# Hybrid DeltaNet/S5 decoder step: a new PSUM allotment, later norm sums and a finer state chain in the mixer of layer 0

## The reference

```python
proj = (h @ w_in).astype(f32)                       # q, k, v, z, b, a
qkv_c, conv_new = short_conv(qkv, conv0, conv_w)    # 4 taps, then silu
q = l2norm(q); k = l2norm(k)
lmat = jnp.where(strict, einsum(kb, kc) * decay, 0.0)
sol = triangular_solve(eye + lmat, rhs)             # w and u of each chunk
qk = einsum(qc, kc) * decay
def step(S, xs):                                    # over the chunks, in order
    v_new = u_i - w_i @ S
    o = (q_i * exp(g_i)) @ S + qk_i @ v_new
    S = S * exp(g_last) + k_dec.T @ v_new
o = rmsnorm(o, norm_g) * silu(z)
out = o @ w_out                                     # then x = x + out
```

## Time and profile before

| | us |
|---|---|
| median of three runs | 4183.62 (4179.11 to 4185.27) |
| profiled execution, its own time | 4190.18 |
| its span | 4188.5 |
| PE busy over the span | 3619.4 (86%) |
| DVE busy | 2147.4 (51%) |
| ACT busy | 849.4 (20%) |
| mixer of layer 0, from 90 to 2110: PE busy | 1708.4 of 2020 |
| the same stretch: DVE busy | 1160.5 |
| the same stretch: mean granted clock of PE | 0.95 |

### The profile page before, as it was taken

The page is one execution under the profiler, slowest core; times in us unless marked ns, Lnnn a source line. Parts: engine busy times, 40 slices in busy tenths (PEclk is TensorE's granted clock), DMA queues, the critical chain, the costliest instruction groups (busy, mean ns, idle before and its releaser), DMA issues.

```text
span 4188.5 us, 56507 instructions
## 1 busy us (share of the span) xinstructions
PE 3619.4 (86%) x23849; PEld 3490.9 (83%) x23849; DVE 2147.4 (51%) x4331; ACT 849.4 (20%) x1691; POOL 846.0 (20%) x773
## 2 busy tenths in 40 slices
PE   4888888888888888878878999999668979999998
PEld 3878878878788888878868999999648969999997
DVE  2564655656556464655646665755561232333334
ACT  2323222232323223222220101011121020000001
POOL 1201011020101101011012332233232313333331
PEclk8989999999999999999988999999868989999998
DMA  2100000010000001000001122222471101111111
GB/s 73 32 21 28 16 32 32 21 33 16 32 27 28 26 26 33 16 32 32 16 27 37 63 74 79 72 81 63 138 216 53 46 26 46 46 46 49 47 46 56
DMA packets 91964, 197.28 MB, mean 47 GB/s; under 512 B 23232, under 2 KB 51008, under 8 KB 90560
## 3 DMA queue, kind: packets, MB, share of 16 engines
q1 hardware_dynamic: 65344, 152.42, 11.4%
q10 hardware_dynamic: 26368, 41.25, 3.0%
HBM read 152.69 MB, written 40.94 MB: 46 GB/s over the span
## 4 chain that ended last, share of the span: by engine, by line
PE 75%; DVE 18%; ACT 2%; issue 2%; DMA 1%; SPq 0%; POOL 0%; DVEq 0%; ACTq 0%; POOLq 0%
PE ps L210 22%; PE ps L467 12%; PE ps L1133 10%; PE ps L546 5%; PE ps L633 4%; PE ps L619 4%; PE ps L629 4%; PE ps L240 2%; PE ps L491 1%; PE ps L485 1%; DVE dwork L1069 1%; PE ps L595 1%; DVE S L1024 1%; PE ps L479 1%; DVE n_r L1342 1%
## 5 line engine op out<-in xcount | busy, mean ns | idle before, releaser
L210 PE MATMUL ps<-hhi,whi 128*128 128x344 f32 x2520 | 811.5, 322 | 86.5 <-DVE hlo L269 71.8
L210 PE MATMUL ps<-hhi,wlo 128*128 128x344 f32 x2520 | 808.8, 321 | 0.0
L210 PE MATMUL ps<-hlo,whi 128*128 128x344 f32 x2520 | 808.1, 321 | 0.0
L1814 POOL TENSOR_TENSOR wtick<-wtick 128x1 f32<-128x1 f32 x213 | 44.0, 206 | 3136.9 <-PE ps L210 977.1
L210 PEld LDWEIGHTS ps<-hhi,whi 128*128 128x128 f32 x2520 | 477.5, 189 | 90.0 <-issue 65.6
L1817 POOL TENSOR_TENSOR wlo<-wraw,whi 128x1024 fp32r<-128x1024 f32 x213 | 534.0, 2507 | 17.1
L210 PEld LDWEIGHTS ps<-hhi,wlo 128*128 128x128 f32 x2520 | 477.0, 189 | 0.0
L210 PEld LDWEIGHTS ps<-hlo,whi 128*128 128x128 f32 x2520 | 476.5, 189 | 0.0
L1186 DVE TENSOR_TENSOR ab<-ps,sg 128x344 f32<-128x344 f32 x132 | 68.2, 517 | 639.2 <-PE ps L210 627.9
L467 PE MATMUL ps<-hhi,whi 128*128 128x344 f32 x1152 | 386.5, 335 | 7.4 <-DVE olo L889 4.6
L467 PE MATMUL ps<-hlo,whi 128*128 128x344 f32 x1152 | 372.2, 323 | 0.0
(11 more groups left out here) (330 smaller groups left out, 6261.7 us busy)
## 6 DMA issues: line engine op xcount, KB each, us to landing
wraw<-in_w SPq DMA_DIRECT2D x213, 512.0 KB, 3.7
tab<-keep_tab SPq DMA_DIRECT2D x8, 1088.0 KB, 6.8
S<-in_sin ACTq DMA_DIRECT2D x16, 512.0 KB, 3.7
out_sout<-S ACTq DMA_DIRECT2D x16, 512.0 KB, 2.6
keep_u<-hs SPq DMA_DIRECT2D x8, 580.0 KB, 3.2
uu<-keep_u SPq DMA_DIRECT2D x8, 580.0 KB, 8.0
keep_tab<-cp ACTq DMA_DIRECT2D x8, 576.0 KB, 6.3
keep_y<-yg SPq DMA_DIRECT2D x64, 68.5 KB, 2.5
```

Of the source, the lines that this page charges most:

```text
L210: ins = nc.tensor.matmul(out, w, r[:, kt, blk(n)], start=k == 0, stop=k == 3 * KT - 1)
```

## The change

- **Banks.** The whole chain has bank 3, with kS and o in columns 0 to 255 and vn and S in columns 256 to 511. Banks 4, 5, 6 and 7 are one pool: each filler states until which slot it will hold its bank, and `aside` takes the bank that is free first by that estimate. In the dense stage `take` goes round seven banks.
- **Chain.** It has eight steps in place of six: o and S are steps of their own. In a quad they stand in slots 0, 1, 2, 3 and 5, 6, 7, 8. In the dense stage steps 0 to 5 lie in the first projection as before, and 6 and 7 in the second; the last gate sum moves from its second half step to its fifth.
- **Norm sums.** `norm(i, 0)` comes after projection 2 instead of 1, `norm(i, 1)` after 3 instead of 2. On DVE the squares of k come before the convolution of q. ACT evacuates projection 2 before the second silu, and makes each root on its own (`root`).
- **DVE's order in a quad.** The level mask of the next quad (`NM` 1) comes before the last add to Y, and the first half of the sample's state update (`sample_add`, k = 0) before `triangle` in slot 9.
- The end of the mixer is written anew for eight chain steps.

```diff
-        DENSE = (0, 1, 2, 5, 6, 7)
-        CHAIN_SLOT = {0: 0, 2: 1, 4: 2, 5: 3, 7: 4, 8: 5}
+        DENSE = (0, 1, 2, 4, 5, 6, 7)
+        CHAIN_SLOT = {0: 0, 1: 1, 2: 2, 3: 3, 5: 4, 6: 5, 7: 6, 8: 7}
...
-            def aside(who, name):
-                nonlocal side
-                side += 1
-                return use(5 + (side - 1) % 2, who, name)
+            def aside(who, name, free_at):
+                b = min(free, key=lambda k: (free[k], k))
+                free[b] = free_at
+                return use(b, who, name)
...
-                    b = use(4, "DVE", g + f"S{c}")
+                else:
+                    p.after("DVE", g + "kd")
+                    b = use(3, "DVE", g + f"S{c}")
...
-                norm(i, 0)
                 for _ in dense_steps(i, 2):
                     pass
-                norm(i, 1)
+                norm(i, 0)
                 p.after("DVE", f"{i}.tab")
                 p.go(rows(i, 0, take, "DVE", f"{i}.0.diff"), f"{i}.0.row")
                 for _ in dense_steps(i, 3):
                     pass
+                norm(i, 1)
...
-                if s == 9 and q + 1 < NQ:
-                    triangle(i, q + 1)
+                if s == 9:
+                    sample_add(i, q, 0)
+                    if q + 1 < NQ:
+                        triangle(i, q + 1)
...
+                        elif q + 1 < NQ:
+                            level_mask(i, q + 1, 1)
```

More of the change, by code:

```diff
@@ L474, in dense_steps, with gate @@
                     yield
-            def gate(g, w, bank):
+            def gate(g, w, bank=take):
                 p.after("DVE", g + "osq")
@@ L554, in slot, with until @@
                 h = SAMPLE_QUAD.get(q)
+                now = (i * NQ + q) * SLOTS + s
+                def until(d):
+                    return lambda who, name: aside(who, name, now + d)
                 if q and s in CHAIN_SLOT:
@@ L557, in slot @@
                 if s == 1:
-                    b = fixed("DVE", g + "ATT")
+                    b = aside("DVE", g + "ATT", now + 1)
                     for c in range(QCH):
@@ L562, in slot @@
                 if s == 2 and q >= 2:
-                    gate(f"{i}.{q - 2}.", QCH * CH, aside)
+                    gate(f"{i}.{q - 2}.", QCH * CH, until(1))
                 if s == 3 and q + 1 < NQ:
-                    p.go(rows(i, q + 1, fixed, "DVE", f"{i}.{q + 1}.diff"), f"{i}.{q + 1}.row")
+                    p.go(rows(i, q + 1, until(1), "DVE", f"{i}.{q + 1}.diff"), f"{i}.{q + 1}.row")
                 if s == 5 and q == NQ - 1:
-                    gate(f"{i}.{NQ}.", B, aside)
+                    gate(f"{i}.{NQ}.", B, until(2))
                 if s == 5 and h is not None:
@@ L584, in slot @@
                         p.after("ACT", f"{i}.silu3")
[L585 removed]
+                    b = aside("ACT", g + "vb", now)
                     for j in range(4):
@@ L597, in slot @@
                 if s == 11:
-                    b = aside("DVE", g + "kd")
+                    b = aside("DVE", g + "kd", now)
                     for c in range(QCH):
@@ L662, in mix_pe @@
             e = HQK - 1
-            gate(f"{e}.{NQ - 2}.", QCH * CH, aside)
-            for k in range(6):
+            gate(f"{e}.{NQ - 2}.", QCH * CH)
+            for k in range(8):
                 chain(e, NQ - 1, k)
                 out_piece(e, k, 0, take)
-            out_piece(e, 6, 0, take)
-            out_piece(e, 7, 0, take)
-            gate(f"{e}.{NQ - 1}.", QCH * CH, take)
+            gate(f"{e}.{NQ - 1}.", QCH * CH)
             for n in (1, 2):
@@ L692, in silu, with root @@
                 a.go(A.activation(qkv[:, t, :], qkv[:, t, :], AF.Silu), f"{i}.silu{t}")
+            def root(i, j):
+                g = f"{i}."
+                for n in range(NC3):
+                    a.after("PE", g + f"nk{j}.{n}")
+                    a.go(A.activation(sqr[j][:, blk(n)], ps[:, a.bank(g + f"ln{j}.{n}"), 0:NB], AF.Ln, bias=eps_t[:, 0:1]), g + f"ln{j}.{n}")
+                a.after("ACT", g + f"ln{j}.{NC3 - 1}")
+                a.go(A.activation(sqr[j], sqr[j], AF.Exp, scale=-0.5), g + f"nr{j}")
             def gate_r(g, w):
@@ L951, in add_x, with sample_add @@
                 v.go(V.tensor_tensor(x[:, m, blk(n)], ps[:, v.bank(f"{e}.x{m}.{n}"), 0:NB], x[:, m, blk(n)], ALU.add), f"{e}.x{m}.{n}")
+            def sample_add(i, q, k):
+                h = SAMPLE_QUAD.get(q)
+                if h is None:
+                    return
+                v.after("PE", f"{i}.drow{h}.{k}")
+                b = v.bank(f"{i}.snew{h}.{k}")
+                for n in range(4):
+                    c = T + 4 * k + n
+                    v.go(V.scalar_tensor_tensor(S0[:, 4 * k + n], ps[:, b, n * P:(n + 1) * P], qkv[:, 0, c:c + 1], S0[:, 4 * k + n], ALU.mult, ALU.add), f"{i}.snew{h}.{k}")
             def slot(i, q, s):
@@ L1041, in mix_dve @@
                     gate_lo(e, NQ - 1)
+                squares(i, 0)
                 conv(i, 1)
-                for j in range(2):
-                    squares(i, j)
+                squares(i, 1)
                 conv(i, 2)
-                for j in range(2):
-                    v.after("ACT", g + f"nr{j}")
-                    v.go(V.scalar_tensor_tensor(qkv[:, j, :], qkv[:, j, :], 1.0 if j == 0 else float(P) ** -0.5, sqr[j], ALU.mult, ALU.mult), g + f"qn{j}")
-                    if j == 0:
-                        decay(i, 0)
+                unit_norm(i, 0)
+                decay(i, 0)
                 conv(i, 3)
+                unit_norm(i, 1)
                 triangle(i, 0)
```

116 lines of the change are left out of this document (57 added, 59 removed).

## The result

| | before | after |
|---|---|---|
| median of 4 runs, us | 4184.44 (4179.11 to 4185.99) | 3982.14 (3981.48 to 3986.41) |
| profiled execution, us | 4190.18 | 3982.19, span 3980.4 |
| ratio, 95% interval | 1 | 0.9521 (0.9504 to 0.9537) |

The kernel became 4.8% faster; the forecast was 3990 us.

A forecast was written before the change was run, and what follows sets the result against it. PE's own work plus its waits for DVE were taken to bound the kernel. Gains 100.2 + 24.5 + 55 + 16 - 2 = 193.7 us; 4190.2 - 193.7 - 6.6 = 3990 us, 4.6% faster, range 3930 to 4060.

The forecast's parts named there:

- Part 1, norm sums: Head of each pair: waits before the norm sums go, 100.2 us, with no new wait at the Gram product.
- the clock term: Norm sums: without waits their products run at full clock, gain 24.5 us, bounds 0 and 24.5.
- Part 2, waits in the quads: Quads: 177.9 us of waits go, 123 us of new ones come, gain 55 us.
- vn of the first chunk (slot 1) needs X, one slot after kS: Quads: new waits of 1.6 us after quads 0 and 2, 0.5 after quad 1; 3.7 a pair.
- the quads' term: Clock in the quads: half of the 33 us lost in slow stretches comes back, 16 us; bounds 0 and 33.
- Part 3, S in o's bank: Chain: S must wait for ACT's copy of o, 0.38 us, but mask products lie between; cost zero.
- the rival with one bank: Chain: S waits for o's copy in full at all 64 products, 24.6 us more, 4015 us; chance 0.07.
- Part 4, end of the mixer: Once, at the mixer's end: second chunk's kS and last gate sum lose cover, some 1 us each, loss 2 us.
- The 6.6 us by which it was moved down: Whole kernel: the profiled execution before lay 6.6 us above the median, so the forecast was lowered by that.
- DVE in the banks' place in full: Quads: gain neither wait nor clock, bank waits only move to vn or a mask; 4061 us, chance 0.16.
- The slower case: Quads: tight chain, each of 48 vn finds a further 4.4 us DVE queue, 211 us, 4201 us; chance 0.03.
- The rival of 3912 us: Quads: new waits are half of those forecast and the clock stays up; chance 0.17.

The follow-up runs named there:

- e1: Kernel before with only the new order of norm sums, squares, roots and multiplications; banks, chain and masks as before: 4053.41 us, ratio 0.9672.
- e3: Kernel after with ACT issuing the sample state's store behind its copy of the next quad's first transpose, not ahead: 3936.45 us, ratio 0.94.
- e2: Kernel after with the norm part undone; one chain bank, pool of four and new mask order stay: 4114.78 us, ratio 0.9827.
- e5: Kernel after with the edits of both e3 and e4: 3915.91 us, ratio 0.9353.
- e4: Kernel after with vn one slot later in both chunks and the steps behind it moved along: 3964.91 us, ratio 0.9467.
- e10: e9 with the second sample update and its store moved into the next quad, the following load also later: 3881.35 us, ratio 0.9272.
- e9: e5 with PE's first transpose of the next quad moved from slot 11 to slot 0, behind kS: 3886.26 us, ratio 0.9283.

## Why the prediction was right, step by step

**Part 1, norm sums: right, the clock term too small.** The waits went in full (100.2 us), and no new one came before the Gram product. The clock term was 24.5 us, and 56.2 - 30.5 = 25.7 came in the sums themselves; another 16 came around them, see the paragraph on the clock. The upper bound was the one to take: with no gap ahead of them, the six products took 1.90 us where they took 3.81. The first sum of the third pair in the kernel after:

```profile
562.95 1.90 PE L481 MATMUL ps<-dwork,ones 128*128 128x344 f32 x6
```

e1 alone gave 133 us where the two terms of the forecast gave 124.7.

**Part 2, waits in the quads: the sum nearly right, one term wrong.** The new waits were put at 123 us. The list has 43.9 + 37.8 + 20.4 + 19.3 + 7.3 + 4.8 and some 7 us of small ones, 141 (the gate sum's 7.4 us are left out, as nearly all of them lie outside the quads, and so is the single wait of 3.8 us, which is the sixteenth case of the first line: it has the same length and place, in the first pair, and is gone in e3). The terms by themselves, third pair:

| step | predicted | measured |
|---|---|---|
| second sample product | 1.3 | 1.38 |
| first transpose, end of quads 0, 1, 2 | 0.8, 1.7, 0.8 | 0.51, 1.72, 0.22 |
| vn slot 6, quads 1, 2, 3 | 2.2, 1.3, 1.3 | 1.61, 1.30, 1.30 |
| vn slot 1 after quad 1 | 0.5 | 0.44 |
| first sample products | 1.0 | 0.90 |
| vn slot 1 after quads 0 and 2 | 1.6 each | none; instead mask products 2.86 each |

Each of these stands on a line like the following, of the kernel after:

```profile
633.44 1.16 PE L598 MATMUL ps<-ident,sdel 128*128 128x128 f32 x8 [1.38 <-DVE S L972]
...
659.76 0.71 PE L520 MATMUL ps<-dwork 128*128 128x128 f32 x4 [1.61 <-DVE dwork L953]
...
694.74 0.71 PE L520 MATMUL ps<-dwork 128*128 128x128 f32 x4 [1.30 <-DVE dwork L953]
```

The step that failed is "vn of the first chunk (slot 1) needs X, one slot after kS". It followed DVE's order up to X, and DVE's part was right: e3, with the store out of the way, shows vn waiting 1.6 us in these 16 places. It didn't follow ACT's queue. There the copy of the first transpose stands behind the issue of the store, and the issue waits for the last sample update. The mask products that need the copy stand one step ahead of vn, so they wait first, and what the prediction gave vn (16 x 1.6 = 25.6 us) is paid there, with 22 us more (43.9 + 3.8 - 25.6). Before, the same order stood in ACT's queue, hidden: PE was held in just that place by a bank that the same update (L1024) kept. Taking away the bank wait made the store's visible. It cost 46 us with its clock (e3).

It could have been read before the change, in the first pair, which has no pieces, and so none that waits for a bank in that place. The kernel before at the start of its quad 1 (L758 is the issue of the store, L713 the copy of the first transpose):

```profile
219.35 0.34 ACTq L758 DMA_DIRECT2D out_sout<-S  x1
219.73 0.60 ACT L713 ACTIVATE dwork<-ps 128x512 f32<-128x512 f32 x1 [4.87 <-DVE S L1024]
...
220.47 1.13 PE L619 MATMUL ps<-dwork 128*128 128x128 f32 x8 [3.81 <-DVE dwork L942]
```

The mask products start behind the copy and wait 3.81 us, in this pair twice. The kernel after has the same two waits of 3.81 us in its first pair. The trace of before names X (L942), which ended last (220.43), but PE started 0.14 us behind the copy's end (219.73 + 0.60 = 220.33), as it did in the kernel after (641.29 + 0.60 = 641.89, then 642.03). Here the prediction read the 2.9 us of the earlier trace rows as the longest wait for DVE in the quads; the list has these two of 3.8 us, in a line that the earlier trace rows leaves out.

**Clock: the quads' term failed, and the norm sums' made up for it.** The place of the clock shows when the mixer is split. The dense stages run from a pair's first projection product to its first mask product, the quads from there to the next pair (the last to the end of the mixer). Sums over the eight stretches (length, then busy times), the dense stages before and after:

```profile
sum 789.83, PE 681.54 PEld 644.91 DVE 359.64 ACT 260.96 POOL 162.53; mean PE 85.19 PEld 80.61 DVE 44.95 ACT 32.62 POOL 20.32
...
sum 643.01, PE 639.79 PEld 622.14 DVE 348.16 ACT 256.27 POOL 156.83; mean PE 79.97 PEld 77.77 DVE 43.52 ACT 32.03 POOL 19.60
```

The quads before and after:

```profile
sum 1236.27, PE 1029.83 PEld 995.08 DVE 802.97 ACT 307.57 POOL 82.03; mean PE 128.73 PEld 124.38 DVE 100.37 ACT 38.45 POOL 10.25
...
sum 1179.68, PE 1026.87 PEld 992.14 DVE 798.19 ACT 309.29 POOL 79.95; mean PE 128.36 PEld 124.02 DVE 99.77 ACT 38.66 POOL 9.99
```

In the quads 16 us were predicted and 3.0 came (1029.83 to 1026.87; 4.1 in e2). In the dense stages 24.5 were predicted and 41.8 came: 25.7 in the norm sums and 16 around them, of which 9.6 in the projections' own products. In e1 it was 37.2 us (681.54 to 644.36). So the price of the waits before the norm sums was more than the slow sums themselves.

The prediction let half of the low clock in the quads go because the new waits around the end of quad 0 would be 3.7 us long. They were 1.38 + 0.51 + 2.86 = 4.75, and in e3 PE was busy 1005.27 us in the quads, 21.6 less than in after. With the cluster as predicted the term would thus have been 1029.83 - 1005.27 = 24.6 us, above the half that I took and inside its bounds of 0 and 33.

**Part 3, S in o's bank: right, no cost.** 64 products, 0.0 us of idle. The Trainium skill (Perfetto Trace Analysis, Optimizing Tensor Performance) has independent groups of matmuls rotate through different PSUM banks. The trace doesn't bear that out for this chain: the 24.6 us of the rival with one bank did not come, and the measurement decides. The likely reason, which is argued and not tried, is that the mask products between o and S cover ACT's copy of o.

**Part 4, end of the mixer: 1.6 us against 2.** kS of the second chunk waited 0.34 us and the last gate sum 1.28.

**The sum.** Idle time of PE in the quads and at the end fell by 53.6 us (206.4 to 152.8), where 55 - 2 were forecast; in the dense stages by 105.1 (108.3 to 3.2), where 100.2 were. With the clock the dense stages gave 146.8 us against 124.7, the quads and the end 56.6 against 69: together 203.4 against 193.7, and some 5 us more behind the mixer, which I did not trace. Taken on profiled executions alone the forecast was 4190.2 - 193.7 = 3996.5 us and 3982.19 came. The 6.6 us by which it was moved down did not apply to the new kernel, whose profiled execution lies on its median. So part of the closeness of 3990 to 3982 is luck: the 12 us that the quads fell short by, for the store on ACT's queue, were balanced by clock around the norm sums that nobody priced.

**The rivals.** DVE in the banks' place in full (4061 us) is excluded by e2, in which the bank half gives 71 us by itself. The slower case needed 4.0 us more before each vn; the longest was 1.6. The single bank had no wait. The rival of 3912 us, half the waits and the clock up, is not what this kernel did, but it is close to what e5 reached (3916) once the store and one slot were out of the way.

## What to carry to other kernels

Before a removed wait is priced, write down for every engine whose result is needed next what stands in its queue, DMA issues included, since an issue that waits for its source holds all that follows it. A wait found at a place covers others at the same place, so the row tells what goes and only the queues tell what comes: here 47.7 us, of which the list of before had shown 7.6 under another name. Look for a part of the program where the covering wait is absent, as in the first pair here: what is hidden elsewhere stands open in it. Price a wait with the clock that goes with it, but for each place by itself: 22 us out of one kind of cluster gave 44 back, 53.6 us out of the quads gave only 3.0 of clock while that cluster stayed.

## What the runs showed of the hardware

- A DMA issue on ACT's queue that waits for its source costs ACT more than the issue itself. The issue took 0.34 us; the copy behind it was held 4.4 us. Moving the 16 issues of this kind behind that copy took 46 us off.
- The clock fell around clusters of waits in which each was under 3 us (0.51, then 2.86, in the third pair, with 1.38 some us ahead), and the stretch of 8 us there had a mean of 0.79. A projection without gaps kept it at 1.00, as this stretch of the kernel after shows:

```profile
580.00:606.00 26.00, 26.00 (x175) 25.98 (x174) 12.68 (x17) 9.08 (x14) 8.71 (x7) 1.00 0.16 46
```

- Low clock does not follow idle time in proportion. From before to after the dense stages lost 105.1 us of idle and 41.8 of busy time, the quads 53.6 and 3.0; e3 took 22.5 and 21.7 off the mixer. e4 had less idle than after (134 us against 156) and was busy longer (1671.0 against 1666.7). e10 had a shorter mixer than e9 and was busy 12.4 us longer behind it, in code that was the same. Why, the runs don't tell.
